# Bias and mask of an attention score: from two matmuls to GpSimd and one VectorE instruction; two other steps moved

## The chip, the cores and the metric

One core of one Trainium2 chip runs the whole program. The metric is device time in microseconds (us), from one launch; lower is better. Engines in the tables: PE is TensorE (matmuls), PEld its weight loads, DVE is VectorE, ACT is ScalarE, POOL is GpSimd, SP is SyncE. SP only issues DMAs here; a q behind an engine's name (SPq) is its queue of issues.

## What is computed

Two transformer blocks in sequence on one sequence of 256 tokens with 1024 features, in float32. The change lies in the second block's mixing layer, in its second attention branch and in the schedule of its neighbours:

```
def fox_attention(q, k, v, f_logit):        # 8 heads of 128
    c = cumsum(log_sigmoid(f_logit), axis=1)                  # per head, one number per token
    s = einsum('bhqd,bkhd->bhqk', q, k) / sqrt(128)
    s = s + c[query] - c[key]
    s = where(kpos <= qpos, s, -inf)
    p = softmax(s, axis=-1)
    return einsum('bhqk,bkhd->bqhd', p, v)
```

Since softmax is taken over the keys, `c[query]` drops out, and what must be added to a row of scores is the bias `-c[key]` and the causal mask. The first branch is a gated linear recurrence (`hgrn2_chunkwise`). The kernel computes it in two halves of four heads: a level of block size 1, 2, 4, ... 64 needs the exponential of a difference of running sums, and a last "cross" level ties chunks together. After the mixing layer comes a cross attention over a memory of 256 tokens.

## The kernel before

Weights come as units of 128 x 2048 numbers (1 MB). SP loads a unit into one of six slots (`raw`), ACT copies it to a rounded part (`high`, L1368), DVE subtracts to get the remainder (`rest`, L1964), and PE multiplies in three products per tile: high x high, rest x high, high x rest (L820, L821, L822, or L857 to L859 where a block goes by tiles). A unit takes PE about 24 matmuls of 512 columns. SP may reload a slot when PE has used its unit; `split_to(n)` in ACT's and DVE's code says up to which unit the two have split the weights at that place.

The mixing layer's weights, `win2`, are 36 units. All engines run a loop over `u` from 0 to 35 with the work of the two branches written between the units:

- **Recurrence, half 0** in u = 8 to 16, half 1 in u = 17 to 25. GpSimd computes the differences of a level (`diff`, L758 and L762) and of the cross level (L745 to L749), ACT their exponentials, DVE the products for keys and queries (L2446, L2449; cross level L2441, L2443, into the buffer `hqk`), PE the scores (L1144, cross level L1156, which is written into the middle of unit 16 or 25), DVE places them (`place_scores`).
- **Attention, head n** in u = 26 + n. After its unit PE writes the scores into a PSUM bank in three steps: a matmul of 384 columns that spreads the bias row over all partitions (L1176), one of 256 columns in bf16 that adds the mask to the two diagonal blocks (L1178), and the score products themselves (L1181). DVE takes the negated row maxima (L2556), ACT the exponentials (L1814). In the next step DVE divides by the sums and transposes in blocks of 32 (`fox_scale`), SP stores the result to DRAM and loads it back turned (`turn_probabilities`, L667 and L663), and three steps on, PE multiplies with the values (`fo`, L1189 and L1190).
- The bias rows `fcum` exist from u = 7. For the matmul they were split into high and remainder on ACT and DVE in u = 8 (`fbias`).
- `load(u)` issues a unit's two DMAs first and then whatever transfer belongs to that place: `turn_fox`, `turn_tokens`, `turn_probabilities`.
- **Behind the loop** comes `brA` (4 units), `brB` (4), `mk` (4), `wout2` (4). DVE normalises the memory tokens, SP turns them over DRAM (`mem_turned`, L648 stores, L654 loads back), and `mk` needs them. `y` (the two branches' sum) and the memory's keys are turned in the same way (`y_turned`, `mem_turned` again).

What sets the order is the order written out by hand, engine by engine, with semaphores between them.

## Time and profile before

| | |
|---|---|
| Median of 3 runs | 1053.22 us (1053.19 to 1053.32) |
| The profiled execution's own time | 1055.78 us |
| Its span (first to last instruction) | 1054.0 us |
| PE busy | 1044.4 us, 99% |
| DVE busy | 756.2 us, 72% |
| ACT busy | 598.8 us, 57% |
| POOL busy | 73.2 us, 7% |
| DMA | 243.89 MB, 231 GB/s over the span |
| Granted TensorE clock | 0.999 of full speed |

A matmul's busy time overlaps that of the next, so 99% busy does not mean that each matmul is at its shortest. What a piece of PE's work costs is read from the distance between the starts of matmuls, and a wait from a row that names a releaser in brackets.

### The profile page before, as it was taken

How to read it: one execution, taken by the hardware profiler on the slowest of the kernel's cores; microseconds unless marked ns; L12 is line 12 of the kernel's file. 1: busy time of each engine (PE TensorE's matmuls, PEld its weight loads, DVE VectorE, ACT ScalarE, POOL GpSimd, SP SyncE). 2: the span in 40 equal slices, each digit the busy share in tenths (PEclk: the TensorE clock that was granted, in tenths of full speed). 3: DMA queues.
4: the chain of work that ended last, by engine and by line, in shares of the span. 5: the costliest groups of instructions: out<-in, count | busy, mean ns of one | idle time of the engine just before them, and what ended most of it. 6: DMA issues, size and time to landing. Idle time of an engine off the chain costs nothing.

```text
span 1054.0 us, 12947 instructions
## 1 busy us (share of the span) xinstructions
PE 1044.4 (99%) x4939; PEld 872.2 (83%) x4939; DVE 756.2 (72%) x901; ACT 598.8 (57%) x800; POOL 73.2 (7%) x59
## 2 busy tenths in 40 slices
PE   9999999999999999999999999999999999999997
PEld 7888888888888888888888888788879988888886
DVE  5768778885787675468988978868778666867642
ACT  6573767764384645447784644554366657565531
POOL 1200000000000000000535500000000000000000
PEclk9999999999999999999999999999999999999999
DMA  9945899985487777557866845889875346777751
GB/s 363 393 129 170 297 291 304 306 261 196 176 278 239 248 224 237 190 203 257 255 192 212 240 160 182 266 275 309 304 261 187 117 165 206 240 241 233 247 163 40
DMA packets 97645, 243.89 MB, mean 231 GB/s; under 512 B 15104, under 2 KB 41904, under 8 KB 97456
## 3 DMA queue, kind: packets, MB, share of 16 engines
q1 hardware_dynamic: 94016, 231.51, 67.8%
q0 software_dynamic: 3136, 11.23, 2.9%
q8 instruction: 39, 0.64, 0.2%
q10 hardware_dynamic: 432, 0.33, 0.1%
q14 instruction: 22, 0.18, 0.0%
HBM read 220.48 MB, written 22.54 MB: 231 GB/s over the span
## 4 chain that ended last, share of the span: by engine, by line
PE 89%; DVE 4%; DMA 3%; ACT 1%; SPq 1%; issue 1%; DVEq 0%; ACTq 0%
PE ps L820 21%; PE ps L822 21%; PE ps L821 21%; PE ps L857 5%; PE ps L859 5%; PE ps L858 5%; DMA y_turned<-y_blocked 2%; DVE rest L1964 1%; PE ps L954 1%; PE ps L1144 1%; PE ps L1253 1%; PE ps L1254 1%; PE ps L1255 1%; DMA mem_turned<-mk_blocked 1%; DMA fpT<-fp_turned 1%
## 5 line engine op out<-in xcount | busy, mean ns | idle before, releaser
L1964 DVE TENSOR_TENSOR rest<-raw,high 128x2048 fp32r<-128x2048 f32 x129 | 295.2, 2304 | 78.2 <-ACT high L1368 77.7
L820 PE MATMUL ps<-high,xt_high 128*128 128x512 f32 x824 | 324.4, 394 | 0.2 <-DVE rest L1964 0.2
L821 PE MATMUL ps<-rest,xt_high 128*128 128x512 f32 x824 | 320.8, 389 | 0.0
L822 PE MATMUL ps<-high,xt_rest 128*128 128x512 f32 x824 | 320.8, 389 | 0.0
L1368 ACT ACTIVATE high<-raw 128x2048 fp32r<-128x2048 f32 x129 | 244.5, 1911 | 74.1 <-DMA raw<-in_units_dram 73.9
L822 PEld LDWEIGHTS ps<-high,xt_rest 128*128 128x128 f32 x824 | 154.7, 188 | 32.5
L820 PEld LDWEIGHTS ps<-high,xt_high 128*128 128x128 f32 x824 | 154.8, 188 | 31.6 <-DVE rest L1964 0.6
L821 PEld LDWEIGHTS ps<-rest,xt_high 128*128 128x128 f32 x824 | 154.8, 188 | 31.1
L1969 DVE SCALAR_TENSOR_TENSOR rest<-raw,wgain,high 128x512 fp32r<-128x512 f32 x176 | 119.0, 746 | 35.5 <-ACT high L1372 35.5
L1372 ACT ACTIVATE high<-raw,wgain 128x512 fp32r<-128x512 f32 x176 | 110.8, 716 | 9.3 <-DMA raw<-in_units_dram 9.3
L1628 ACT ACTIVATE act<-ps,recips 128x256 f32<-128x256 f32 x44 | 18.4, 470 | 85.1 <-PE ps L822 85.0
L822 PE MATMUL ps<-high,ht_rest 128*128 128x512 f32 x168 | 65.4, 389 | 0.0
L821 PE MATMUL ps<-rest,ht_high 128*128 128x512 f32 x168 | 65.4, 389 | 0.0
L820 PE MATMUL ps<-high,ht_high 128*128 128x512 f32 x168 | 65.4, 389 | 0.0
L857 PE MATMUL ps<-high,xt_high 128*128 128x512 f32 x152 | 60.6, 399 | 1.3 <-DVE rest L1964 1.3
L859 PE MATMUL ps<-high,xt_rest 128*128 128x512 f32 x152 | 59.4, 391 | 0.0
L858 PE MATMUL ps<-rest,xt_high 128*128 128x512 f32 x152 | 59.2, 390 | 0.0
L1388 ACT ACTIVATE xt_high<-ps 128x512 fp32r<-128x512 f32 x26 | 15.2, 598 | 58.7 <-PE ps L954 53.3
L2313 DVE SCALAR_TENSOR_TENSOR hid<-ps,recips,act 128x256 f32<-128x256 f32 x44 | 19.2, 479 | 39.7 <-ACT act L1628 39.6
L821 PEld LDWEIGHTS ps<-rest,ht_high 128*128 128x128 f32 x168 | 31.5, 188 | 6.6
L820 PEld LDWEIGHTS ps<-high,ht_high 128*128 128x128 f32 x168 | 31.5, 188 | 6.5
L822 PEld LDWEIGHTS ps<-high,ht_rest 128*128 128x128 f32 x168 | 31.5, 188 | 6.5
(372 smaller groups left out, 1450.6 us busy)
## 6 DMA issues: line engine op xcount, KB each, us to landing
raw<-in_units_dram SPq DMA_DIRECT2D x350, 512.0 KB, 4.9
gv_turned<-gv_blocked SPq DMA_DIRECT2D x11, 512.0 KB, 6.1
gv_t<-gv_turned SPq DMA_DIRECT2D x44, 128.0 KB, 3.6
turned<-blocked SPq DMA_DIRECT2D x22, 256.0 KB, 5.3
hid_t<-turned SPq DMA_DIRECT2D x88, 64.0 KB, 4.2
fox_turned<-fqT SPq DMA_DIRECT2D x6, 512.0 KB, 3.1
raw<-in_units_dram SPq DMA_DIRECT2D x8, 256.0 KB, 4.7
fqT<-fox_turned SPq DMA_DIRECT2D x16, 128.0 KB, 4.6
```

What stands on the lines that cost most here:

```text
L820: pe.matmul(out, sh, wh, start=first, stop=False)
L821: pe.matmul(out, sh, wr, start=False, stop=False)
L822: mm = pe.matmul(out, sr, wh, start=False, stop=last)
L857: pe.matmul(out, sh, wh, start=first, stop=False)
L858: pe.matmul(out, sh, wr, start=False, stop=False)
L859: mm = pe.matmul(out, sr, wh, start=False, stop=last)
L1368: act.activation(high[:, u % SLOTS, c], raw[:, u % SLOTS, c], ACT.Copy).then_inc(unit_high, 1)
L1372: ins = act.activation(high[:, u % SLOTS, c], raw[:, u % SLOTS, c], ACT.Copy, scale=g[:, k:k + 1])
L1628: act.activation(act_[:, j % 2, tt, :], gate_values[:, tt, :], ACT.Silu, scale=recips[:, c:c + 1])\
L1964: vec.tensor_tensor(rest[:, slot, c], raw[:, slot, c], high[:, slot, c].bitcast(F32), ALU.subtract).then_inc(unit_rest, 1)
L1969: ins = vec.scalar_tensor_tensor(rest[:, slot, c], raw[:, slot, c], g[:, q:q + 1], high[:, slot, c].bitcast(F32), ALU.mult, ALU.subtract)
L2313: ins = vec.scalar_tensor_tensor(hid[:, j % 2, :, tt, :], fold(values[:, tt, :]), recips[:, c + tt:c + tt + 1], fold(act_[:, j % 2, tt, :] ...
```

## The change

1. **Bias and mask.** The two matmuls L1176 and L1178 go, for all 8 heads, and with them the constants `identr` and `identb` (a DVE instruction and a DMA) and the preparation of `fbias` in u = 7 and 8 (two ACT and three DVE instructions). In their place SP stores the bias rows to DRAM once (`store_biases`, two DMAs in u = 13 of the loads). GpSimd spreads each head's row over the 128 partitions with a DMA of 192 KB (`spread_bias`) and adds the mask to the diagonal blocks (`mask_bias`, 128 x 256), one head ahead. On DVE the maximum becomes one instruction that computes bias - score, writes it back to PSUM and reduces it with min; ACT's exponential takes it with scale -1.
2. **Probabilities ahead of loads.** `turn_probabilities` is called first in `load(u)`, and stores and loads back the same head there. Before, the store of head h stood behind the load of unit 32 + h and the loading back behind that of unit 33 + h.
3. **Half 1's first difference** waits for the cross level of half 0 (`(0, 128)`); before, it waited for the level of block size 64.
4. DVE splits three units ahead from u = 9 on (before, four or five from u = 21 on), ACT three from u = 26 on (before, five), so that two units' split falls behind the loop.
5. The stores of the memory tokens count on one semaphore for both tiles (`mem_stored`), so each loading back waits for both; the gate of u = 33 waits for both stores of `oa_turned` instead of one.

The core of the diff:

```
         def load(u):
+            turn_probabilities(u)
             slot = u % SLOTS
 ...
             turn_tokens(u)
-            turn_probabilities(u)
+            store_biases(u)
 ...
+        def store_biases(u):
+            if u == UNIT["win2"] + 13:
+                sync.wait_ge(sem("fcum_ready"), 1)
+                for c0, w in ((0, P), (P, S)):
+                    sync.dma_start(fcum_dram[:, c0:c0 + w], fcum[0:HH, 0:w]).then_inc(fcum_stored, 16)
 ...
         def turn_probabilities(u):
-            h = u - UNIT["win2"] - 33
+            h = u - UNIT["win2"] - 32
             if 0 <= h < HH:
+                sync.wait_ge(fp_blocked, h + 1)
+                sync.dma_start(fp_turned[h], fpT[:, h % 3, :]).then_inc(fp_stored, 16)
                 sync.wait_ge(fp_stored, 16 * (h + 1))
 ...
-            h += 1
-            if 0 <= h < HH:
-                sync.wait_ge(fp_blocked, h + 1)
-                sync.dma_start(fp_turned[h], fpT[:, h % 3, :]).then_inc(fp_stored, 16)
 ...
-                turn(u, UNIT["brA"] + 9, mem_turn, tt, mem_blocked[:, tt, :])
+                turn(u, UNIT["brA"] + 9, mem_turn, tt, mem_blocked[:, tt, :], stored_at=16 * TT)
 ...
                 if lv == LEVELS[0]:
                     pool.wait_ge(sem("hb_ready"), hf + 1)
                     if hf:
-                        pool.wait_ge(sem("level_ready"), applied(HG_STEPS.index((0, 64))))
-                elif lv == LEVELS[1]:
-                    if hf:
                         pool.wait_ge(sem("level_ready"), applied(HG_STEPS.index((0, 128))))
 ...
+        def spread_bias(h):
+            if h == 1:
+                pool.wait_ge(aux_done, AUX["lv", 1, 128, 0][0] + 1)
+            elif h == HALF + 1:
+                pool.wait_ge(aux_done, AUX["fs", HALF - 1][0] + 1)
+            elif h:
+                pool.wait_ge(sem("fox_max"), TT * (h - 1))
+            pool.dma_start(bias_home(h)[:, :], fcum_dram[h].partition_broadcast(P)).then_inc(fbias_landed[h % 2], 16)
+        def mask_bias(h):
+            pool.wait_ge(fbias_landed[h % 2], 16 * (h // 2 + 1))
+            d = bias_home(h)[:, :].rearrange("p (n c) -> p n c", n=3)[:, 0:3:2, :]
+            pool.tensor_tensor(d, d, causal[:, :, :], ALU.add).then_inc(fbias_masked, 1)
 ...
+                    for h in range(HH + 1):
+                        if h < HH:
+                            spread_bias(h)
+                        if h:
+                            mask_bias(h - 1)
 ...
         def fox(n):
             if n < HH:
                 out = aux(("fs", n))
-                pe.matmul(out[:, 0:P + S], identr[:, n:n + 1].to_broadcast([P, P]), fbias[:, :], start=True, stop=False)
-                diagonal = out[:, 0:P + S].rearrange("p (n c) -> p n c", n=3)[:, 0:3:2, :]
-                pe.matmul(diagonal, identb[:, :], causal[:, :, :], start=False, stop=False)
 ...
-            split_to(UNIT["win2"] + u + 5)                             # ACT
+            split_to(UNIT["win2"] + u + (5 if u < 26 else 3))
 ...
-                split_to(UNIT["win2"] + u + (4 if 5 < u < 9 or 20 < u < 23 else 3 if 8 < u < 21 else 5))   # DVE
+                split_to(UNIT["win2"] + u + (5 if u < 5 else 4 if u < 9 else 3))
 ...
+                    vec.wait_ge(fbias_masked, n + 1)
                     for tt in range(TT):
                         c0, c1 = (0, P) if tt == 0 else (P, P + S)
-                        ins = vec.tensor_reduce(small["negmax"][:, n, tt:tt + 1], src[:, c0:c1], AX_X, ALU.max, negate=True)
-                        ins.then_inc(sem("fox_max"), 1)
+                        vec.tensor_tensor_reduce(src[:, c0:c1], src[:, c0:c1], bias_home(n)[:, c0:c1], -1.0, -3 * NEG,
+                                                 ALU.add, ALU.min, small["negmax"][:, n, tt:tt + 1])\
+                            .then_inc(sem("fox_max"), 1)
```

What the diff alone does not show is where the moved instructions stand on their engines. On GpSimd, at the seam of the two halves, before (L762 computes a level's difference, L758 that of block size 64):

```order
L758 TENSOR_TENSOR he<-hb 128x2x4x64 [waits level_ready]
L762 TENSOR_TENSOR he<-hb 128x1024 [waits level_ready,hb_ready]
L762 TENSOR_TENSOR he_next_123<-hb 128x1024 [waits level_ready]
L745 TENSOR_TENSOR crossref<-hb 128x4
L746 TENSOR_TENSOR he_cross_125<-hb 128x4x64
```

and after (L775 is the level's difference now):

```order
L771 TENSOR_TENSOR he<-hb 128x2x4x64 [waits level_ready]
L775 TENSOR_TENSOR he<-hb 128x1024 [waits level_ready,hb_ready]
L775 TENSOR_TENSOR he_next_121<-hb 128x1024
L758 TENSOR_TENSOR crossref<-hb 128x4
L759 TENSOR_TENSOR he_cross_123<-hb 128x4x64
```

The order stays; the first of half 1 now waits for a later count, and the second waits for nothing more.

On SP, from the store of head 1's probabilities on, before (L603 loads a unit, L667 stores probabilities, L663 loads them back turned):

```order
L667 DMA fp_turned<-fpT 128x384 [waits fp_blocked]
L603 DMA raw<-in_units_dram 128x1024 [waits unit_used]
L603 DMA raw<-in_units_dram 128x1024
L648 DMA oa_turned<-oa_squares 128x1024 [waits oa_blocked]
L663 DMA fpT<-fp_turned 32x4x96 [waits fp_stored]
L663 DMA fpT<-fp_turned 32x4x96 x3
L667 DMA fp_turned<-fpT 128x384 [waits fp_blocked]
```

and after (L611 loads a unit, L676 stores, L680 loads back):

```order
L676 DMA fp_turned<-fpT 128x384 [waits fp_blocked]
L680 DMA fpT<-fp_turned 32x4x96 [waits fp_stored]
L680 DMA fpT<-fp_turned 32x4x96 x3
L611 DMA raw<-in_units_dram 128x1024 [waits unit_used]
L611 DMA raw<-in_units_dram 128x1024
L676 DMA fp_turned<-fpT 128x384 [waits fp_blocked]
```

Loading back has moved ahead of a unit's load and ahead of the store of `oa_turned`; each unit's load now stands behind the wait for that step's probabilities and for their store.

On DVE, behind the loop, before (L2651 finishes the gates, L2652 takes head 7's output, L2672 is the first product with `brA`):

```order
L2651 TENSOR_SCALAR gate_135<-gate_135 128x2048 [waits gate_tanh]
L2652 COPY fo<-ps 128x256 [waits aux_done]
L2672 TENSOR_TENSOR gate_134<-gate_134,ps 128x2x512 [waits unit_used,vector_steps]
L2660 TENSOR_TENSOR xt_rest<-fo,xt_high 128x512 [waits fo_high] x4
L1964 TENSOR_TENSOR rest<-raw,high 128x2048 [waits unit_high] x2
```

and after:

```order
L2669 TENSOR_SCALAR gate_133<-gate_133 128x2048 [waits gate_tanh]
L2670 COPY fo<-ps 128x256 [waits aux_done]
L1988 TENSOR_TENSOR rest<-raw,high 128x2048 [waits unit_high,vector_steps]
L1988 TENSOR_TENSOR rest<-raw,high 128x2048 [waits unit_high]
L2690 TENSOR_TENSOR gate_132<-gate_132,ps 128x2x512 [waits unit_used]
```

Two units' remainders have moved in between the copy and the gate product; ACT has their two high parts ahead of `xt_high<-fo` in the same way.

## Rows read from the trace of the kernel before

**Rows 1.** The page, part 1: busy time, share of the span, instructions
```profile
PE 1044.4 (99%) x4939; PEld 872.2 (83%) x4939; DVE 756.2 (72%) x901; ACT 598.8 (57%) x800; POOL 73.2 (7%) x59
```

**Rows 2.** PE's longest wait: who waited for whom, us in total, times, longest
```profile
PE ps L857 <- DVE rest L1964: 1.3, 1, 1.3
```

**Rows 3.** Timeline of PE at head 6: start us, us, engine, line, instruction
```profile
674.51 0.34 PE L1176 MATMUL ps<-fbias,identr 128*128 128x384 f32 x1
674.69 0.28 PE L1178 MATMUL ps<-causal,identb 128*128 128x256 bf16 x1
674.81 0.82 PE L1181 MATMUL ps<-fkT,fqT 128*128 128x128 f32 x4
...
676.35 0.39 PE L821 MATMUL ps<-rest,xt_high 128*128 128x512 f32 x1
```

**Rows 4.** Timeline of PE one head earlier; in brackets idle time and its releaser
```profile
667.02 0.82 PE L1181 MATMUL ps<-fkT,fqT 128*128 128x128 f32 x4
668.28 0.70 PE L1189 MATMUL ps<-fpT,fv 128*128 128x256 f32 x2 [0.44 <-DMA fpT<-fp_turned]
...
669.27 0.39 PE L821 MATMUL ps<-rest,xt_high 128*128 128x512 f32 x1
```

**Rows 5.** Timeline of PE at the cross level, half 0, then half 1
```profile
559.37 0.39 PE L822 MATMUL ps<-high,xt_rest 128*128 128x512 f32 x1
560.63 1.16 PE L1156 MATMUL ps<-hqk 128*128 128x128 f32 x8 [0.87 <-DVE hqk L2443]
561.54 0.48 PE L820 MATMUL ps<-high,xt_high 128*128 128x512 f32 x1
...
621.23 0.39 PE L822 MATMUL ps<-high,xt_rest 128*128 128x512 f32 x1
...
622.27 0.48 PE L820 MATMUL ps<-high,xt_high 128*128 128x512 f32 x1
```

**Rows 6.** Timeline of DVE and POOL there; the last row is half 1's
```profile
555.49 3.81 POOL L762 TENSOR_TENSOR he<-hb 128x1024 f32<-128x1024 f32 x1 [13.45 <-DVE hqk L2449]
...
555.26 2.28 DVE L1964 TENSOR_TENSOR rest<-raw,high 128x2048 fp32r<-128x2048 f32 x1
557.46 2.38 DVE L2441 TENSOR_TENSOR hqk<-he_cross,hk 128x512 f32<-128x512 f32 x1
...
618.92 0.69 DVE L2441 TENSOR_TENSOR hqk<-he_cross,hk 128x512 f32<-128x512 f32 x1 [0.74 <-PE ps L1144]
```

**Rows 7.** Timeline of SP, and the chain that ended last, before 668 us
```profile
659.48 2.08 SPq L663 DMA_DIRECT2D fpT<-fp_turned  x4
...
661.13 7.10 DMA fpT<-fp_turned
```

**Rows 8.** 640 to 700 us: busy time by engine, clock, DMA share, GB/s
```profile
640.00:700.00 60.00, 59.56 (x282) 48.90 (x281) 53.40 (x81) 29.88 (x48) 0.00 (x0) 1.00 0.82 246
```

**Rows 9.** Groups by line and shape, DVE and POOL: busy us, mean ns, idle before
```profile
L2600 DVE SCALAR_TENSOR_TENSOR gate<-ps,recips,gains 128x512 f32<-128x512 f32 x8 | 5.6, 742 | 0.0
...
L2556 DVE TENSOR_REDUCE negmax<-ps 128x1 f32<-128x256 f32 x8 | 3.3, 412 | 0.0
...
L2556 DVE TENSOR_REDUCE negmax<-ps 128x1 f32<-128x128 f32 x8 | 2.3, 282 | 0.0
...
L746 POOL TENSOR_TENSOR he_cross<-hb 128x256 f32<-128x256 f32 x2 | 1.2, 608 | 0.0
```

**Rows 10.** Timeline of DVE behind the loop
```profile
707.30 1.22 DVE L2672 TENSOR_TENSOR gate<-gate,ps 128x1024 f32<-128x1024 f32 x1 [5.11 <-PE ps L822]
```

**Rows 11.** Timeline of SP: the memory tokens stored and loaded back
```profile
719.31 1.47 SPq L648 DMA_DIRECT2D mem_turned<-mem_blocked  x2
...
728.05 3.65 SPq L654 DMA_DIRECT2D mem_blocked<-mem_turned  x8
```

**Rows 12.** The chain that ended last, 739 to 775 us, its first piece
```profile
732.78 8.60 DMA y_turned<-y_blocked
```

**Rows 13.** Windows, columns as in Rows 8, while these transfers run
```profile
728.00:732.00 4.00, 4.00 (x20) 3.30 (x19) 2.94 (x3) 0.38 (x1) 0.00 (x0) 1.00 1.00 293
```

More of the change, by code:

```diff
@@ L366, in build @@
         at_rest = place("at_rest", [P, KC, S], F32R, area)
-        fbias = place("fbias", [P, P + S], F32R, area + 62 * KB)
+        fbias = [place(f"fbias{n}", [P, P + S], F32, area + k * KB) for n, k in enumerate((62, 28, 54))]
         junk_m = place("junk_m", [P, TT, NB], F32, area + 8 * KB)
@@ L474, in build, with bias_home @@
         eps_ready = sem("eps_ready")
+        fcum_dram = nc.dram_tensor("fcum_rows", (HH, P + S), F32, kind="Internal").ap()
+        fcum_stored, fbias_masked = sem("fcum_stored"), sem("fbias_masked")
+        fbias_landed = [sem(f"fbias_landed{n}") for n in range(2)]
+        def bias_home(h):
+            return fbias[0 if h % 2 == 0 else 1 + h // HALF]
         fox_blocked, fox_stored = sem("fox_blocked"), sem("fox_stored")
@@ L1738, in _ @@
                     fox_log_sigmoids()
-                if u == 8:
-                    act.wait_ge(sem("fcum_ready"), 1)
-                    for c0, w in ((0, P), (P, S)):
-                        act.activation(fbias[0:FROWS, c0:c0 + w], fcum[:, 0:w], ACT.Copy).then_inc(sem("fcum_high"), 1)
                 if u == 5:
@@ L2533, in _ @@
                     vec.wait_ge(aux_taken[AUX["flog", 1][1]], AUX["flog", 1][2] + 1)
-                    step(vec.memset(fbias[:, :].bitcast(F32), 0.0))
                     settle()
```

42 lines of the change are left out of this document (17 added, 25 removed).

## Prediction

> **What bounds the kernel now.** I read the page's first part, then PE's waits, then the chain of waits, and last the timelines of the places where the change cuts in. PE is busy 1044.4 of 1054.0 us [rows 1], so time can only go where PE has an instruction less or a wait less, and can only come where PE gets a new wait. The waits are few: the longest is 1.3 us at L857 [rows 2], and the two that lie in the changed code are one of 0.44 us for turned probabilities [rows 4] and one of 0.87 us at the cross level of half 0 [rows 5]. All other engines have room on average, but between 640 and 700 us, where the heads are processed, DVE is busy 53.40 of 60 us and the DMA engines 82% [rows 8]; there the question is who is late, not who is busy.
>
> **Two matmuls per head.** The cost of a matmul is the distance between starts, since busy times overlap. From the start of L1176 at 674.51 to that of L1181 at 674.81 [rows 3] the bias and the mask take 0.30 us of PE, in all eight heads alike. Without them L1181's weights load under the unit's last product, as those of L1176 did. 8 x 0.30 = **2.4 us**, all on the path, since PE is the path. The sum of the busy times (0.34 + 0.28) would say 5.0 us and be wrong, for the reason above. The least it can be is nothing like zero: 640 columns per head are simply not streamed. I keep 2.2 to 2.6.
>
> **The wait for probabilities.** At head 2's output PE starts L1189 1.26 us behind L1181 and the next unit's second product 2.25 us behind it (669.27 - 667.02) [rows 4]; where nothing waits, the latter is 1.54 us (676.35 - 674.81) [rows 3]. So this wait costs **0.7 us**, more than the 0.44 in brackets. The chain shows what ended it: the transfer back, 7.10 us to 668.23 [rows 7]; its four DMAs were issued from 659.48 on, behind a whole unit's load and behind that of the recurrence's output. After the change the store and the loading back go ahead of that load and a step (some 7 us: 674.81 - 667.02 less this wait) earlier: the wait for the store and four issues, then the landing. Even at 7.10 us it is there before PE asks. What is late next is the unit's load: it now stands behind the probabilities' wait, their store and four issues of together some 2 us. A slot filled in this way is split by ACT three units later and used by PE five units later, so a delay of 5 or 10 us meets a cover of two to three steps. I take 0.7 whole.
>
> **The cross level.** From the last product of the unit's first half to the first of its second, half 0 takes 2.17 us (561.54 - 559.37) and half 1 1.04 us (622.27 - 621.23) for the same eight matmuls [rows 5]: **1.1 us** are waiting. PE waits for DVE's L2443, which stands behind L2441, and that took 2.38 us where half 1's took 0.69 [rows 6]. Beside it runs GpSimd's first difference of half 1, 555.49 to 559.30: DVE's L1964 ran from 555.26 to 557.54 at its usual length, GpSimd's work was stretched meanwhile, and then DVE stood until GpSimd was done. The change puts that difference behind L2443, so L2441 runs alone and L2443 is done near 558.9, before PE asks at 559.6. The difference then lies beside DVE's copies out of PSUM, and half 1's first level is needed by ACT only in u = 17, after half 0's outputs and one more unit; two differences of at most 3.81 us each are there by then. I take 1.1, with 0.5 as the low end if something else of DVE stands in the way by then.
>
> The page "SBUF — State Buffer" of the Trainium skill, section "Who interferes with whom", has the rule for this: GpSimd shares a pair of SBUF ports with VectorE, whoever issues first keeps it for the whole instruction, and a VectorE instruction with two SBUF inputs contends with a GpSimd one that reads SBUF. By that rule the trace agrees with the gain here, and the same rule speaks against the new masks on GpSimd, which is the second rival below.
>
> **New work on DVE.** The trace has no instruction that adds, writes PSUM and reduces. Its floor is the two reductions that it replaces, 0.28 + 0.41 = 0.69 us per head; its ceiling two instructions of the next larger shape, 2 x 0.742 = 1.48 us [rows 9]. That is 0 to 0.8 us more per head, and I take 0.4, as the shapes are nearer to the reductions': 3.2 us over the heads, against 60.0 - 53.4 = 6.6 us free [rows 8], and with no high part of ACT ahead of the exponentials the heads start some 2 us earlier. On the path: nothing. If that cover were gone, it would come out 1:1.
>
> **New work on GpSimd and on its queue.** Per head a DMA of 192 KB and an addition of 128 x 256, 0.61 us by L746 [rows 9]. DVE's new wait (`fbias_masked`) has the unit splits behind it, and behind those PE. The mask of head n is queued behind the spreading for n + 1, which waits for head n - 1's maximum; DVE writes a unit's remainder first (2.28 us [rows 6]) and then that maximum, so it is done some 3 us into a step of 7, and 4 us are left for an issue and a mask of 0.61. The row itself is issued nearly two steps ahead. On the path: nothing, unless that landing takes 9 us or more. The preparation in u = 7 and 8 that goes, and the store of the bias rows that comes, lie under PE with no wait near them.
>
> **Two splits behind the loop.** DVE gets 2 x 2.28 us in a stretch where it sat idle for 5.11 [rows 10]: it fits with 0.5 us to spare, and the gate product, which starts the memory tokens' chain, keeps its place. ACT gets two high parts there too and has about as much room.
>
> **One semaphore for both memory tokens' stores.** The stores were issued within 1.47 us from 719.31 on, and the first loading back began at 728.05, when the first store had landed [rows 11]. It must now wait for the second: 0 to 1.1 us later. SP issues in order, so what is queued behind is the next unit's load and the store `y_turned` at 732.78, right after the eight issues' end at 731.70 and one load. With that store begins the chain (8.60 us for its first piece [rows 12], then the second, then the keys) that ends in PE's wait at L857 [rows 2], with no slack. So up to 0.9 us come back there. But the DMA engines are full (share 1.00 [rows 13]), and a transfer issued later into a full queue does not land as much later. I take **0.4 us lost**, between 0 and 0.9.
>
> **Sum.** 2.4 + 0.7 + 1.1 - 0.4 = 3.8 us gained. The profiled execution took 1055.78 us with a span of 1054.0, 2.6 us above the median of 1053.22; I take the differences as they are to the median: 1053.2 - 3.8 = **1049.4 us** (span near 1050.2).
>
> **Rivals.**
> *The chain behind the loop takes more back.* Unit loads that SP now issues later pile up near 695 us, before the memory's own 1 MB, and everything from there to L857 hangs on full DMA engines. For it: the share of 1.00 and a wait at L857 that is there already. Against it: that chain is started anew by DVE's gate products, in step with PE. If it slips by 1 to 2.5 us, and that comes out at L857: 1050.5 to 1052. The same price if one of the two waits stays or comes back in another place.
> *Masks against splits.* If GpSimd holds DVE for each mask, 8 x 0.61 = 4.9 us, and with 0.8 us per new instruction another 6.4: 11.3 us against 6.6 free, 2 of head start and some 4 of slack that a unit's remainder has before PE needs it (it is written two units of 5.5 us ahead, less DVE's own work of a step; an estimate). That just holds; I price what may come through at 0 to 1.5 us: 1049.4 to 1051. By the port rule of the page named above it would be this case, if it is any.
> *Slower: the bias comes late.* Bias rows of even heads share a buffer, so a landing, an issue, a mask and a maximum must fit into two steps, 14 us. With some 5 us for everything but the landing, it begins at 9 us, and a transfer of 7.10 us stands in this very stretch [rows 7]. At 13 us DVE falls back 4 us per pair of heads, 12 us over the three pairs that follow, less the slack of 4 and less the gains: 1053.2 - 3.8 + 8 = 1057.4. It decides from 11.6 us on, where it only eats the gain (3 x 2.6 - 4 = 3.8).
> *The DMA phase turns out kinder.* If the transfers behind L857 fall better, part of its 1.3 us goes too: 1048.3.
>
> **How the numbers follow.** Forecast, 1048.8 to 1050.3: 0.58. Kinder phase, below 1048.8: 0.12. The chain or the masks take more, 1050.3 to 1052: 0.22, of which about half is past 1051.1. The bias late: 0.08, half of it near 1053, half above 1055.3. A measurement of this kernel can tell about 0.2%, 2.1 us, from no change: faster means below 1051.1, slower above 1055.3. So faster 0.58 + 0.12 + 0.12 = 0.82, same 0.14, slower 0.04. The range of 8 in 10 leaves out the slow end and a little below: 1048.2 to 1051.5.
>
> **What the profile after would show.** L1181's start 0.22 to 0.23 us behind the unit's last product in all eight heads; no row of PE with `fpT<-fp_turned` as releaser; the cross level of half 0 at 1.04 us and L2441's successor at 0.69; GpSimd's first difference of half 1 beside copies out of PSUM. The new DVE pair between 0.7 and 1.5 us. PE's wait at L857 between 1.3 and 2.3 us: if it is longer, the chain behind the loop took it. Wrong would be: a wait of PE for a remainder (`rest`) between 640 and 700 us, an idle time of DVE that `fbias` ends, or an unchanged distance at the cross level.

## The result: slower by 1.4%, and the profile after

The changed kernel takes 1068.41 us (median of 4 runs, 1066.60 to 1068.78), against 1053.20 of the kernel before (4 runs). The ratio is 1.0139, 95% interval 1.0127 to 1.0151. The prediction, 1049.4 and faster, is wrong in its direction. The profiled execution took 1068.36 us with a span of 1066.2.

The waits of PE, as in [rows 2]: who waited for whom, us in total, times, longest.

```profile
PE ps L1219 <- DMA fpT<-fp_turned: 8.2, 4, 3.2
PE ps L890 <- DVE rest L1988: 3.8, 1, 3.8
...
PE ps L853 <- DVE mt_rest L2707: 0.4, 1, 0.4
```

The wait for turned probabilities, which the change was said to remove, went from 0.4 to 8.2 us. (L1219 was L1189, L890 was L857, L1988 was L1964, L1211 was L1181, L1189 is now the cross level, L853 to L855 are L820 to L822.) The page's busy times answer to [rows 1]: PE has 2.4 us more although it has 16 instructions less, and DVE is not busier.

```profile
PE 1046.8 (98%) x4923; PEld 874.1 (82%) x4923; DVE 755.0 (71%) x913; ACT 598.3 (56%) x798; POOL 83.6 (8%) x74
```

**Where the gains are.** The cross level of half 0, timeline of PE, against [rows 5]: 560.32 - 559.28 = 1.04 us where 2.17 stood, the 1.1 us that were predicted.

```profile
559.28 0.39 PE L855 MATMUL ps<-high,xt_rest 128*128 128x512 f32 x1
559.51 1.05 PE L1189 MATMUL ps<-hqk 128*128 128x128 f32 x8
560.32 0.48 PE L853 MATMUL ps<-high,xt_high 128*128 128x512 f32 x1
```

Timelines of DVE and of POOL there, against [rows 6]: DVE's cross level products take 0.69 us each, and the first difference begins behind them and takes 1.89 us, not 3.81. The contention did not vanish, it moved: DVE's next remainder takes 3.57 us beside GpSimd, where no PE waits for it.

```profile
557.39 0.69 DVE L2464 TENSOR_TENSOR hqk<-he_cross,hk 128x512 f32<-128x512 f32 x1
558.12 0.69 DVE L2466 TENSOR_TENSOR hqk<-he_cross,hq 128x512 f32<-128x512 f32 x1
...
561.28 3.57 DVE L1988 TENSOR_TENSOR rest<-raw,high 128x2048 fp32r<-128x2048 f32 x1
...
558.96 1.89 POOL L775 TENSOR_TENSOR he<-hb 128x1024 f32<-128x1024 f32 x1 [16.94 <-DVE hqk L2466]
```

From head to head the scores start every 6.11 us, later 6.80, where they were 6.44 and 7.08 apart: 0.3 us per head, as predicted. At head 7 they start at 677.52, in the kernel before at 681.89: **4.4 us are won by then**.

**Where they are lost.** The outputs of heads 4 and 5 in PE's timeline, two of the slowed matmuls behind the second, and the wait behind the loop; in brackets the idle time and its releaser. (Heads 6 and 7 wait 1.10 and 1.32 us more.)

```profile
680.86 0.70 PE L1219 MATMUL ps<-fpT,fv 128*128 128x256 f32 x2 [2.52 <-DMA fpT<-fp_turned]
...
690.47 1.22 PE L1219 MATMUL ps<-fpT,fv 128*128 128x256 f32 x2 [3.23 <-DMA fpT<-fp_turned]
...
694.47 0.63 PE L853 MATMUL ps<-high,xt_high 128*128 128x512 f32 x1
694.90 0.63 PE L854 MATMUL ps<-rest,xt_high 128*128 128x512 f32 x1
...
784.60 0.47 PE L890 MATMUL ps<-high,xt_high 128*128 128x512 f32 x1 [3.80 <-DVE rest L1988]
```

The last head's output is at 708.45 where it was at 700.91. So between the last scores and the last output 7.5 + 4.4 = 11.9 us are lost: 8.2 of waiting, and most of the rest is PE's clock. Behind the wait of 3.23 us matmuls of 512 columns start 0.43 us apart instead of 0.23, until 696.2. The view by stretches says the same (stretch, its length, busy time and instructions of PE, its weight loads, DVE, ACT and POOL, then granted clock, DMA share, GB/s): the granted clock is 0.50 from 691 to 696 us, that is the level of 1.2 GHz, 0.97 over the next five, and 1.00 from 701 on.

```profile
686.00:691.00 5.00, 1.77 (x7) 1.19 (x6) 2.58 (x7) 2.80 (x6) 0.00 (x0) 0.85 0.48 113
691.00:696.00 5.00, 5.00 (x14) 3.99 (x13) 2.75 (x2) 0.86 (x1) 0.00 (x0) 0.50 0.95 310
...
701.00:706.00 5.00, 5.00 (x24) 4.18 (x24) 4.93 (x6) 2.47 (x2) 0.00 (x0) 1.00 0.58 210
```

Behind the loop another 4.7 us go (the last matmul is at 1060.22, before at 1047.99; 12.2 us in all, less the 7.5 by which head 7's output is late): 2.4 more at L890 than at L857 before (3.80 against 1.35), some 1.6 of lower clock right behind it, 0.4 at the memory tokens.

**Who is late.** SP's timeline (start, duration of the issues; q is the queue of issues) over two heads:

```profile
652.17 0.33 SPq L676 DMA_DIRECT2D fp_turned<-fpT  x1
...
659.24 0.43 SPq L656 DMA_DIRECT2D oa_turned<-oa_squares  x1
659.72 0.43 SPq L676 DMA_DIRECT2D fp_turned<-fpT  x1
666.62 1.75 SPq L680 DMA_DIRECT2D fpT<-fp_turned  x4
668.40 0.91 SPq L611 DMA_DIRECT2D raw<-in_units_dram  x2
669.36 2.41 SPq L662 DMA_DIRECT2D hg<-oa_turned  x4
671.81 0.47 SPq L676 DMA_DIRECT2D fp_turned<-fpT  x1
677.65 1.73 SPq L680 DMA_DIRECT2D fpT<-fp_turned  x4
679.42 0.90 SPq L611 DMA_DIRECT2D raw<-in_units_dram  x2
680.37 0.43 SPq L656 DMA_DIRECT2D oa_turned<-oa_squares  x1
680.84 0.43 SPq L676 DMA_DIRECT2D fp_turned<-fpT  x1
...
699.87 0.43 SPq L676 DMA_DIRECT2D fp_turned<-fpT  x1
```

From head 2 on, each store is issued within 2.5 us behind a unit's two loads, while these still run, and SP stands until it has landed (666.62 - 659.72 = 6.9 us, 677.65 - 671.81 = 5.8). At heads 3 to 6 a transfer of the recurrence's output (`oa_turned` or `hg`, 512 KB) stands between too, and SP stands for 5.0 to 6.9 us; at heads 2 and 7, with the load alone ahead, for 4.3 and 5.3. The chain of waits has that landing as its largest piece between 635 and 715 us (28.3%):

```profile
652.17 4.31 DMA fp_turned<-fpT
...
659.72 6.88 DMA fp_turned<-fpT
...
680.84 6.38 DMA fp_turned<-fpT
```

From the store of head 2 (652.17) to that of head 7 (699.87) SP needs 47.7 us, **9.5 us per head, where PE needs 6.80**. So SP falls back by some 2.7 us with each head. With the median of 1.9 us to land, head 1's probabilities are there at about 651, more than 6 us before PE multiplies with them (657.77), head 2's some 5 us before (664.57), head 3's only 1.5 (671.37); at head 4 the slack of about one step is gone. From there PE runs at SP's pace. Once, for head 5, the chain goes another way round: over `hg`, which SP issued late as well (5.95 us to land), ACT's `at_high`, DVE's `at_rest` and the blocks; SP is free for the store at the same moment. The first two heads show nothing of it, because there SP still waits for DVE's blocks before it stores, and the unit's load has landed meanwhile.

### The profile page after: what moved, and what is told of

It reads as the page before. It is cut to its first block, busy times and chain, and to the rows that moved or that the text cites. A ratio compares the mean times of both kernels' runs of the same rounds, so it can differ in the third digit from the quotient of the medians.

```text
span 1066.2 us, 12952 instructions
## 1 busy us (share of the span) xinstructions
PE 1046.8 (98%) x4923; PEld 874.1 (82%) x4923; DVE 755.0 (71%) x913; ACT 598.3 (56%) x798; POOL 83.6 (8%) x74
## 4 chain that ended last, share of the span: by engine, by line
PE 86%; DMA 7%; DVE 3%; SPq 2%; ACT 1%; issue 1%; DVEq 0%; ACTq 0%
PE ps L853 20%; PE ps L855 20%; PE ps L854 20%; PE ps L890 5%; PE ps L892 5%; PE ps L891 5%; DMA fp_turned<-fpT 2%; DMA raw<-in_units_dram 1%; PE ps L987 1%; PE ps L1177 1%; DMA mem_turned<-mk_blocked 1%; DMA mem_turned<-mem_blocked 1%; SPq L662 1%; PE ps L1282 1%; PE ps L1281 1%; PE ps L1280 1%
## 5 line engine op out<-in xcount | busy, mean ns | idle before, releaser
L1988 DVE TENSOR_TENSOR rest<-raw,high 128x2048 fp32r<-128x2048 f32 x129 | 295.6, 2305 | 76.6 <-ACT high L1395 76.0
L853 PE MATMUL ps<-high,xt_high 128*128 128x512 f32 x824 | 325.4, 395 | 0.2 <-DVE rest L1988 0.2
L855 PE MATMUL ps<-high,xt_rest 128*128 128x512 f32 x824 | 321.5, 390 | 0.0
L855 PEld LDWEIGHTS ps<-high,xt_rest 128*128 128x128 f32 x824 | 155.2, 188 | 32.7
L853 PEld LDWEIGHTS ps<-high,xt_high 128*128 128x128 f32 x824 | 155.4, 189 | 32.0 <-DVE rest L1988 0.6
L853 PE MATMUL ps<-high,ht_high 128*128 128x512 f32 x168 | 65.4, 389 | 0.0
L855 PE MATMUL ps<-high,ht_rest 128*128 128x512 f32 x168 | 65.4, 389 | 0.0
L890 PE MATMUL ps<-high,xt_high 128*128 128x512 f32 x152 | 61.3, 403 | 3.8 <-DVE rest L1988 3.8
L892 PE MATMUL ps<-high,xt_rest 128*128 128x512 f32 x152 | 60.1, 395 | 0.0
L890 PEld LDWEIGHTS ps<-high,xt_high 128*128 128x128 f32 x152 | 29.0, 191 | 9.8 <-issue 4.2
L855 PEld LDWEIGHTS ps<-high,ht_rest 128*128 128x128 f32 x168 | 31.5, 188 | 6.6
```

What stands on the lines that cost most here:

```text
L853: pe.matmul(out, sh, wh, start=first, stop=False)
L855: mm = pe.matmul(out, sr, wh, start=False, stop=last)
L890: pe.matmul(out, sh, wh, start=first, stop=False)
L892: mm = pe.matmul(out, sr, wh, start=False, stop=last)
L1988: vec.tensor_tensor(rest[:, slot, c], raw[:, slot, c], high[:, slot, c].bitcast(F32), ALU.subtract).then_inc(unit_rest, 1)
```

## The experiments

Their results in one table. Medians are of the runs that were compared; the ratio is to the kernel before on the same chip, with its 95% interval. "Output" is the start of PE's first product behind the heads (`at_high`), and "last" that of its last matmul, both in the profiled execution; before: 695.4 and 1048.0.

| kernel | median us | ratio | output | last |
|---|---|---|---|---|
| after | 1068.41 | 1.0139 (1.0127 to 1.0151) | 701.4 | 1060.2 |
| a_prob_behind | 1053.87 | 0.9999 (0.9985 to 1.0014) | 691.8 | 1045.0 |
| b_prob_ahead | 1073.99 | 1.0186 (1.0161 to 1.0211) | 714.5 | 1068.3 |
| b_first_diff | 1052.11 | 0.9983 (0.9973 to 0.9994) | 693.3 | 1044.2 |
| b_no_bias | 1053.81 | 1.0000 (0.9986 to 1.0013) | 694.1 | 1046.8 |
| a_store_ahead | 1050.91 | 0.9981 (0.9972 to 0.9990) | 690.7 | 1043.3 |
| a_back_next | 1051.13 | 0.9984 (0.9975 to 0.9993) | 691.1 | 1043.1 |
| a_all_behind | 1068.35 | 1.0138 (1.0124 to 1.0151) | 705.0 | 1060.3 |
| a_ahead_splits_back | 1063.85 | 1.0100 (1.0084 to 1.0115) | 700.4 | 1054.1 |
| b_diff_store_ahead | 1059.41 | 1.0059 (1.0046 to 1.0071) | 700.1 | 1052.7 |
| b_diff_splits_ahead | 1051.64 | 0.9987 (0.9978 to 0.9995) | 692.6 | 1044.3 |
| a_ahead_act_splits | 1050.56 | 0.9976 (0.9966 to 0.9985) | 690.4 | 1041.8 |
| b_diff_no_bias | 1050.96 | 0.9986 (0.9977 to 0.9995) | 690.8 | 1043.1 |
| a_two_sems | 1051.62 | 0.9989 (0.9980 to 0.9998) | 691.8 | 1043.2 |
| a_ahead_two_sems | 1051.82 | 0.9987 (0.9977 to 0.9997) | 692.9 | 1045.8 |

### One part undone, one part alone

**a_prob_behind**: after, with the probabilities' turn back behind the loads (part 2 undone).

```
         def load(u):
-            turn_probabilities(u)
 ...
+            turn_probabilities(u)     # back of h - 1, then store of h, as before
```

> The changed kernel with its second part alone undone: the store of a head's probabilities stands behind the load of unit 32 + h again, and the loading back behind that of unit 33 + h. Everything else of the change stays. Queue theory (SP waits for its own store with nothing in between, so that a head costs SP 8 to 11 us where PE's step is 7): the loss goes as a whole, PE waits for no turned probabilities except perhaps 0.7 us once, and what is left is the gain of the two matmuls and of the cross level less up to 0.9 us behind the loop: 1049 to 1050.5 us. Bias theory (GpSimd's rows and masks, or the unit splits that come later now, hold DVE): SP's order changes little, 1060 us or more. Both: something in the middle, 1053 to 1058.

Measured: ratio 0.9999; PE waits 0.6 us for turned probabilities and 1.4 at the unit that goes by tiles (L892, the former L857). The whole loss is part 2's. But the rest of the change, for which 1049 to 1050.5 us were expected, gives nothing that can be told from the kernel before.

**b_prob_ahead**: before, with part 2 alone.

> The kernel before with the second part alone: probabilities stored and loaded back ahead of the unit's load. Bias and mask stay matmuls, the splits stay five units ahead. Queue theory: SP's cycle per head is that of the changed kernel, store wait 5 to 7 us, four issues 1.75, a load 0.95, every second head another 2.4; PE waits for fpT in the last heads and the clock drops behind the longest wait: 1065 us or more, and more than the changed kernel if ACT, which wants a unit two steps earlier here, waits for the late loads ahead of its exponentials. Bias theory: under 1055.

Measured: ratio 1.0186, worse than the whole change. PE waits 8.2 us for `at_rest`, 4.9 for the exponentials and 3.5 for turned probabilities. The time is in the range that was expected, but by another way: here the store lands in 2.7 us (median), not in 5 to 7, and SP waits for DVE's blocks ahead of seven of the eight stores (in after, of four), so this is not after's loop; the waits of DVE between 630 and 730 us show another, which the runs on the splits below take apart:

```profile
DVE rest L1962 <- ACT high L1366: 31.5, 9, 5.1
```

**b_first_diff**: before, with part 3 alone.

> The kernel before with the third part alone: half 1's first difference waits for the cross level of half 0. Both theories: L2441 at 0.69 us instead of 2.38, the cross level of half 0 takes PE 1.04 us instead of 2.17, and 1.1 us are gained, unless the wait for probabilities or the one at L857 takes some of it back: 1052.0 to 1052.6 us.

Measured: ratio 0.9983, 1.8 us by the medians, 1.1 expected. The wait at the cross level is gone, and in the profiled execution those at L1189 and L857 too.

**b_no_bias**: before, without the two matmuls and with nothing in their place (bias and mask are left out).

```
-                pe.matmul(out[:, 0:P + S], identr[:, n:n + 1].to_broadcast([P, P]), fbias[:, :], start=True, stop=False)
-                diagonal = out[:, 0:P + S].rearrange("p (n c) -> p n c", n=3)[:, 0:3:2, :]
-                pe.matmul(diagonal, identb[:, :], causal[:, :, :], start=False, stop=False)
-                pe.matmul(diagonal, identb[:, :], causal[:, :, :], start=False, stop=False)
```

> The kernel before without the two matmuls for bias and mask (so bias and mask are left out of the scores), everything else as it was. Both theories: 8 x 0.30 us of PE go, 1050.8 us, if the two waits that are there stay as they are; the wait for probabilities of head 2 may change by some tenths, as that chain runs on DVE and SP. If the time per head is not 0.30 but 0.6 (busy times), 1048.3.

Measured: ratio 1.0000 instead of 0.9977. Head by head the 0.3 us are there, but the wait for turned probabilities goes from 0.4 to 1.6 us, and at the heads' end 1.2 us are left in the profiled execution; in the medians nothing can be seen.

```profile
PE ps L1186 <- DMA fpT<-fp_turned: 1.6, 1, 1.6
PE ps L857 <- DVE rest L1961: 1.2, 1, 1.2
```

PE came to that wait 1.9 us earlier (its scores there start at 665.16 instead of 667.02); the transfer landed only some 0.7 earlier, so that the output starts at 667.62 instead of 668.28. What is waited for there is set by SP and the DMA engines.

### What holds SP: the store behind the load

**a_store_ahead**: after, with the unit's load between the store and the wait for it.

```
         def load(u):
-            turn_probabilities(u)
+            store_probabilities(u)    # wait for the blocks, store
 ...
             store_biases(u)
+            land_probabilities(u)     # wait for the store, load back
```

> The changed kernel with one thing different: in each step SP first issues the probabilities' store, then the unit's load, then whatever else belongs there, and only then waits for the store and loads back. Theory (SP's queue waits for its own store, which lands behind the 1 MB load issued just before): the store no longer has that load ahead of it, the wait that holds SP shrinks from 4.3 to 6.9 us to 1 to 3 us, SP's cycle per head falls to PE's step of 6.8 us, PE's waits for turned probabilities fall from 8.2 us to under 2, and the time is 1050 to 1056. Rival 1 (the DMA engines are so full that a store takes 4 us or more wherever it stands, and any wait for it in the same step costs that): SP's cycle stays above 8 us and the time between 1058 and 1068. Rival 2 (what costs is that the wait for DVE's blocks stands ahead of a load): as rival 1, but with SP waiting for fp_blocked and not for the store.

Measured: ratio 0.9981, and 17.5 us less than after by the medians. PE waits for no probabilities at all; its longest waits are:

```profile
PE ps L896 <- DVE rest L1994: 1.3, 1, 1.3
PE ps L1018 <- DVE warmth L2149: 1.1, 1, 1.1
```

The page's part on DMAs (size, median us from issue to landing), first of after, then of a_store_ahead:

```profile
fp_turned<-fpT SPq DMA_DIRECT2D x8, 192.0 KB, 5.1
fpT<-fp_turned SPq DMA_DIRECT2D x32, 48.0 KB, 1.9
```

```profile
fp_turned<-fpT SPq DMA_DIRECT2D x8, 192.0 KB, 2.8
fpT<-fp_turned SPq DMA_DIRECT2D x32, 48.0 KB, 3.7
```

The order of issue decides who stands behind the megabyte. In after it is the store, for which SP waits; in a_store_ahead it is the loading back, for which nobody waits until PE does, a step later (head 4's is issued at 670.49, its output starts at 677.82). SP's step is then PE's: the store of head 4 is at 665.26, that of head 5 at 672.87, head 6 at 678.93, 6.8 us apart on average.

```profile
665.26 0.34 SPq L677 DMA_DIRECT2D fp_turned<-fpT  x1
665.64 1.98 SPq L611 DMA_DIRECT2D raw<-in_units_dram  x2
...
670.49 1.75 SPq L686 DMA_DIRECT2D fpT<-fp_turned  x4
672.87 0.34 SPq L677 DMA_DIRECT2D fp_turned<-fpT  x1
...
678.93 0.34 SPq L677 DMA_DIRECT2D fp_turned<-fpT  x1
```

The page "DMA: Bandwidth & Descriptors" of the Trainium skill, section "Queues, rings and completion order", says that each DMA engine takes an issuing engine's descriptors in the order of its ring. The landings of 5.1 against 2.8 us agree with it.

**a_back_next**: after, with the loading back of head h - 1 and then the store of head h both ahead of the load, a step apart.

> The changed kernel with the loading back of head h-1 and the store of head h both ahead of the unit's load, a step apart: a store has a whole step of 6.8 us to land before SP waits for it. Theory (what costs is the wait for the store in the same step, not the place ahead of the load): no wait of PE for turned probabilities above 0.5 us, SP's cycle equal to PE's step, at_high's products start near 691 us, and the time is 1 to 3 us below the version with the probabilities behind the loads (span 1049 to 1050.5). Rival (any wait ahead of the loads delays them, or the loading back comes later than with the store a step earlier and PE waits for it): PE's wait for fpT 1 us or more, or waits for rests, and no gain against the version behind the loads.

Measured: ratio 0.9984, PE's wait for probabilities 0.2 us. (The interval overlaps that of a_prob_behind, so the 1 to 3 us expected against that version are not shown.) To stand ahead of the load is harmless if the store has a step's time to land.

**a_all_behind**: after, with the three steps (store, wait, loading back) together, but called behind the load.

```
         def load(u):
-            turn_probabilities(u)
 ...
             store_biases(u)
+            turn_probabilities(u)     # store, wait and back of h, unchanged
```

> The changed kernel with the probabilities' three steps (store, wait for the store, loading back) kept together in one step of SP, but called behind the unit's load and not ahead of it. Theory (what costs is a store issued right behind a 1 MB load and waited for at once): the order round the loop is the same as in the changed kernel, so the store lands 4 to 7 us after its issue in most heads, SP's cycle is 8 us or more again, and the time is 1060 to 1070. Rival (what costs is that the load stands behind the wait): each load goes out one wait earlier, the stores land as late but PE waits for nothing more than 1 us, and the time is 1050 to 1055.

Measured: ratio 1.0138, the same as after. The store's landing has a median of 5.8 us (5.2 at the two last heads, where the load alone is ahead of it), and PE waits for probabilities 10.3 us. So it isn't the load's late issue that costs: with each load issued one wait earlier the time is the same. It is the store that stands right behind a load and is waited for at once.

### What the splits have to do with it

**a_ahead_splits_back**: a_store_ahead, with the splits where the kernel before has them (part 4 undone). **b_diff_store_ahead**: the kernel before with part 3 and the same order of SP, the two matmuls kept.

```
-            split_to(UNIT["win2"] + u + (5 if u < 26 else 3))                 # ACT
+            split_to(UNIT["win2"] + u + 5)
-                split_to(UNIT["win2"] + u + (5 if u < 5 else 4 if u < 9 else 3))   # DVE
+                split_to(UNIT["win2"] + u + (4 if 5 < u < 9 or 20 < u < 23 else 3 if 8 < u < 21 else 5))
```

> The version with the store ahead of the load, with DVE's and ACT's splits at the places of the kernel before. Theory (the later splits only make room for the new instruction and cost nothing): PE waits for a rest or a maximum in the heads by up to 2 us, since DVE has 1.1 us of new work per head and no room made for it, and the time is 1051 to 1053. Rival (the later splits are what gives back 1 to 2 us behind the loop): the time is 1049.5 to 1050.5 and mk starts as early, with no wait at the tiles' unit.

> The kernel before with the first difference of half 1 moved and the probabilities' store ahead of the unit's load (loading back behind it, in the same step), and with the two matmuls as they were. Theory (the two matmuls cost 0.3 us per head, 2.4 in all, and nothing but PE limits the heads once no wait is left): at_high's products start 2.4 us later than the 690.7 of the same version with the new bias, at 693.0 to 693.3, and the time is 1 to 2.5 us above its 1050.9. Rival (GpSimd's and DVE's new work take back as much as the matmuls cost): within 0.5 us of 1050.9.

Measured: 1.0100 and 1.0059, both far from either expectation: I had taken the splits' place for a matter of 1 to 2 us. The store lands well here (1.9 us). The chain of waits between 640 and 710 us of a_ahead_splits_back closes on itself:

```profile
663.19 0.34 SPq L677
663.57 0.43 SPq L611
664.04 7.04 DMA raw<-in_units_dram
671.11 1.92 ACT high L1401
...
675.26 0.29 DVE ps L2585
675.61 0.32 DVE ps L2585
676.00 1.27 DVE gate L2630 x2
...
678.26 0.90 ACT fp L1844 x4
679.39 0.56 DVE fp L2120 x2
679.97 0.59 DVE fpT L2122
680.58 0.34 SPq L677
```

Store, load, its landing, ACT's high part, DVE's remainder, the maximum, the exponentials, the blocks, and the next store: 680.58 - 663.19 = 17.4 us for two heads, where PE's own steps are 2 x 6.80 = 13.6 (two units are loaded in one turn). With splits five units ahead the unit whose load waited for the blocks of one step is the unit that the next step's split wants, and the next blocks stand behind that split.

**b_diff_splits_ahead**: b_diff_store_ahead with part 4 (the gate of u = 33 waits for both stores of `oa_turned`, which the later splits need). **a_ahead_act_splits**: a_store_ahead with ACT's splits alone back at five.

> The kernel before with the first difference of half 1 moved, the probabilities' store ahead of the unit's load, and the later splits of the changed kernel (DVE three units ahead from u = 9, ACT three from u = 26, and the gate of u = 33 waiting for both stores of oa_turned); the two matmuls of bias and mask as before. Theory (with splits five ahead, a load that waits for the heads' blocks is needed by the split of the very next step, and load, ACT, DVE, blocks, next load become a loop of 16.2 us for two heads; three ahead opens it): the 1059.4 us of the same kernel with the old splits fall to 1051.5 to 1053.5, no wait of PE for at_rest or fpT above 1 us, at_high's products start at 692.6 to 693.5. Rival (it was the two matmuls, or DVE's load in the heads, that made that kernel slow): it stays above 1056. Second question, what the new bias is worth: by 0.30 us per head this kernel should be 2.4 us above the version with the new bias and the same queue order, measured as 0.9981 of the kernel before, so 0.9995 to 1.0012 of it; the rival (worth nothing in time) 0.997 to 0.999.

> The changed kernel with the store ahead of the load, and only ACT's splits back at five units ahead (DVE's stay at three). Theory (the loop closes at the first engine that waits for the unit just loaded, and ACT's exponentials stand behind its split): ACT waits for raw units at the heads as with both splits back, the exponentials and with them the blocks come late, and the time is 1058 to 1065. Rival (only DVE's split, which stands ahead of the maxima and the blocks, closes it): ACT waits for raw, but the time stays at 1051 to 1053.

Measured: 0.9987 and 0.9976. Part 4 alone takes 7.8 us off b_diff_store_ahead, so it opens the loop, with the old bias too. In the second kernel ACT does wait for raw units, and nothing comes of it; I had expected the loop to close there. Waits of ACT, 630 to 715 us:

```profile
ACT high L1401 <- DMA raw<-in_units_dram: 20.8, 9, 5.3
```

So ACT's split alone doesn't close the loop; it takes DVE's, which stands ahead of the maxima and the blocks. In this kernel's profiled execution PE's wait at L896 is gone too (whether through ACT's earlier high parts was not taken apart), and its median is the lowest of all versions: **1050.56 us against 1053.16**, beside 1068.41 of after. Its interval overlaps that of a_store_ahead, so the difference between these two isn't shown.

### What the bias is worth, and the shared semaphore

**b_diff_no_bias**: before, with part 3 and without the two matmuls (bias and mask left out).

> The kernel before with the first difference of half 1 moved and without the two matmuls of bias and mask (both left out, nothing in their place). Theory (both gains are PE's own and add, and the wait for probabilities takes back what SP's pace allows): at_high's products start 3.0 to 3.8 us before the kernel before's 695.4, with 0 to 1 us waiting for fpT, and the time is 1050.5 to 1052. Rival (from the heads on the pace is set by SP's loads and DMA engines, so PE's gains come back as waits): the time stays at 1052 or above, the wait for fpT is 1.5 us or more or a wait for a rest stands behind the loop.

Measured: ratio 0.9986. In the profiled executions the product behind the heads starts 2.5 us before that of b_first_diff (690.83 against 693.29), and the last matmul 1.2 us before (1043.06 against 1044.22): half of the gain is given back behind the loop, 0.9 us in a wait for the memory tokens. In the ratios (0.9986, b_first_diff 0.9983) none of the 2.4 us can be seen. b_diff_splits_ahead against a_store_ahead, which has the new bias at the same order, says the same: 1.9 us at the heads' end (692.57 against 690.66), 1.0 at the last matmul, where L896 waits 1.3 us and its like in the other 0.3. The ratios, 0.9987 and 0.9981, are 0.6 us apart, within their intervals: 0.9987 lies in the range that was expected if the new bias is worth nothing in time (0.997 to 0.999), not in that for 2.4 us. A worth of 0.3 us per head is seen in the heads of every trace; in the time of the whole kernel it is not shown.

**a_two_sems**: a_prob_behind with a semaphore for each of the memory's two stores. **a_ahead_two_sems**: the same on a_store_ahead.

```
-        mem_turn = (sem("mem_blocked"), 2 * [sem("mem_stored")], [sem(f"mem_landed{n}") for n in range(2)],
+        mem_turn = (sem("mem_blocked"), [sem(f"mem_stored{n}") for n in range(2)], [sem(f"mem_landed{n}") for n in range(2)],
```

> The changed kernel with the probabilities back behind the loads, and the memory tokens' two stores counted on a semaphore each, as in the kernel before (the bias rows' store counts on the semaphore of fcum_ready instead, to have one free). Theory (the shared semaphore delays the chain behind the loop by 0 to 0.9 us, as predicted): the distance from the first product of mk to the last matmul falls from 308.9 us to 308.0 to 308.9, and PE's wait of 1.4 us for the rest at L892 with it. Rival (the 2.3 us that this version loses behind the loop against the kernel with only the first difference moved come from the full DMA engines' phase or from the later splits): the distance stays at 308.5 to 309.5 and the time within 1 us of 1053.9.

> The version with the store ahead of the load and the loading back behind it, with the memory tokens' stores on two semaphores again (as in the kernel before). Theory (the shared semaphore costs some tenths in the chain behind the loop): the wait of 1.3 us at the first rest product of the tiles' unit shrinks or goes, and the time is 0.3 to 1 us below that version's 1050.9. Rival (that wait comes from the DMA engines' phase, which is another in every version): within 0.3 us of 1050.9, the wait of any size from 0 to 1.5 us.

Measured: 0.9989 where a_prob_behind had 0.9999, and 0.9987 where a_store_ahead had 0.9981. The two differences have opposite signs and lie within the intervals. From the first product of `mk` to the last matmul a_two_sems takes 306.8 us where a_prob_behind took 308.9, and the wait of 1.4 us at L892 is gone; in the other pair it is 308.2 against 308.3, with 1.1 us of wait against 1.3. So the two pairs disagree, and whether the shared semaphore costs the 0.4 us that I took stays open. In a_ahead_two_sems' profiled execution a wait of 1.7 us for probabilities stands that the same queue order did not have in a_store_ahead; single executions differ by that much.

## Why the prediction was wrong

**The step that failed** is in "The wait for probabilities": "the wait for the store and four issues, then the landing", priced for the unit's load, with the store itself, as "together some 2 us". Four issues are 1.75 us, so this left 0.3 for the store to land. It took 5.1 us (median). The row for it was there: [rows 7] has a transfer of 48 KB pieces that took 7.10 us behind a unit's load, in this very stretch. I used it for the loading back, and not for the store, which the change put into just that place. What mattered was not how long it is but who waits for it: before, a step and a load lay between the store and its wait; after, nothing.

**The second failure is that the delay was treated as a fixed one.** "A delay of 5 or 10 us meets a cover of two to three steps" was right for each single load: PE waited for no remainder in the heads. But SP's step became 9.5 us where PE's is 6.80, and a cover does not hold against a pace. The sum to make was SP's own round: 5.1 landing, 1.75 back, 0.91 load, and 0.43 or 2.41 for the recurrence's output, with waits. With the landing measured here it gives 8 to 10 us per head. PE's waits for probabilities, put at nothing, became 8.2 us. None of the rivals had SP as the bound; the one on the slower side was about the bias row, whose landing was 3.4 to 6.4 us, far from the 11.6 from which it decides.

**The clock** was no part of any case. Of the 11.9 us lost in the heads some 3, and of the 4.7 behind them 1.6, are PE at 0.50 of its clock behind the waits of 3.23 and 3.80 us.

Point by point, of the rest:

- **Two matmuls.** The 0.3 us per head were right, in every kernel (steps of 6.11 and 6.80 us without the two matmuls, 6.44 and 7.08 with them). "All on the path, since PE is the path" was not: in the profiled executions about half comes back as waits behind the loop or for a transfer (b_no_bias, b_diff_no_bias), and in the ratios of the same two kernels nothing of it can be seen. The chain of the memory tokens and of `y` goes at the pace of DVE and the DMA engines, so the waits shown in [rows 2] are not a constant.
- **Cross level.** Mechanism and size right: 2.17 - 1.04 = 1.13 us.
- **DVE's new instruction.** 0.30 and 0.47 us, and 0.14 for each read of the accumulator: 1.05 us per head, 0.36 more than the reductions; 0.4 was taken. It cost nothing on the path.
- **Masks.** 0.69 to 2.61 us, median 0.86, for 0.61 taken. The longest, from 652.25, lies beside DVE's remainder (652.07 to 654.32) and ends 0.6 us behind it. DVE's waits in the heads name no mask, and no wait of PE came from one.
- **Two splits behind the loop.** Right that they fit. But "no cost" missed what they do: they give SP's loads two more steps, without which the same change of the queue costs 8 to 13 us (b_diff_store_ahead against b_diff_splits_ahead, a_ahead_splits_back against a_store_ahead).
- **The base.** "I take the differences as they are to the median" took waits of one execution as waits of the median. The profiled execution of before held waits at L1189 and L857 of some 2 us that its median run, 2.6 us shorter, seems not to have: a_store_ahead has neither of the two matmuls, nor the wait for probabilities, nor that at the cross level, and its last matmul is 4.7 us ahead of that of the profiled execution, but its median only 2.1 us ahead of the median. That the difference is just these waits was not shown, as only one execution of before has a trace here.
- **The chain behind the loop.** As in the first rival, SP came out of the heads late, with 14 DMAs of loads to issue in one piece (706.91 to 726.57), and L890 waited 3.8 us. That it follows from SP's delay isn't shown: in a_all_behind SP came out of the heads later still (710.70), and that wait was 1.5 us.

## What to carry to other kernels

When a DMA is moved on a queue that waits for its own transfers, make the sum of that queue's whole round (issues, and each landing that is waited for, taken from rows of a transfer behind what will now stand ahead of it) and hold it against the step of the engine that bounds the kernel: a slack of steps covers a delay, not a pace. Put the store ahead of the large load and the wait for it behind, so that what stands behind the megabyte is what nobody waits for yet. And follow a load's release round: if its condition is an output of the step whose successor needs that very load, the prefetch depth in use is zero, however many slots there are; here splitting less far ahead was what made room.

## What the runs showed of the hardware

- 192 KB on SP's queue land in a median of 1.9 to 3.4 us in the kernels where the unit's load of 1 MB is mostly not right ahead of them or has had time to land, and of 5.1 and 5.8 us (up to 6.9 and 7.6) where it is (after, a_all_behind). In half of these heads 512 KB of the recurrence's output stand ahead too; with the load alone it is 4.3 to 5.3 us. In turn the four pieces of 48 KB land in a median of 3.3 to 4.3 us where a load stands ahead of them, and of 1.9 to 2.0 where SP waited in between for a store that it had issued behind that load (after, a_all_behind, b_prob_ahead).
- Behind two single waits of PE the granted clock was 0.50: after 3.23 us of waiting from the first matmul on (690.47), for 5.7 us; after 3.80 us (784.60) from the third matmul on (785.16), for 3.4 us. The matmuls of 512 columns start 0.43 us apart there. The wait of 2.52 us at 680.86 was followed by a clock of 1.00.
- GpSimd's difference and DVE's remainder share out as a lock would: in the kernel before GpSimd came second and took 3.81 us, after the change DVE came second at 561.28 and took 3.57 us for 2.28, with 1.4 us of GpSimd's instruction (560.81, 1.89 us long) still to run. The rule of the page "SBUF — State Buffer" of the Trainium skill, section "Who interferes with whom", has it this way, and the trace agrees in both directions.
